# VectorE's order of work in the mixed attention heads: maxima first, row sums and pair splits one step later, a quarter of the next weights split early

## The reference, cut to what matters

```
x += diff_attention(rms_norm(x)) ; x += sq_relu_mlp(rms_norm(x))      # layer 0
k, v = shared_kv(x)
x += swa_sink_attention(rms_norm(x), k, v) ; x += sq_relu_mlp(...)    # layer 1

# diff_attention, 8 heads, S = 1024 rows in 8 blocks of 128; per head:
q, k = rms_norm of each 64 wide half of h @ w_qkv;  v = 128 wide
p_c = softmax(q_c k_c^T - slope*dist, chunk-causal)        # c = 0, 1
o = (p_0 - lam * p_1) @ v ;  o = rms_norm(o) * (1 - lambda_init)
```

## Time and profile before

| | us |
|---|---|
| median of 3 runs | 2393.85 (2392.53 to 2394.03) |
| the profiled execution | 2394.06 |
| its span, first to last instruction | 2392.3 |
| start of the first and of the last projection matmul into `proj` (layer 0) | 46.1 and 522.5 |
| PE busy in the span | 2231.4 (93%) |
| DVE busy | 1591.2 (67%) |
| ACT busy | 1156.5 (48%) |
| POOL busy | 832.6 (35%) |

### The profile page before, as it was taken

One profiled execution on the slowest core, in us unless ns is written; L12 is line 12 of the kernel. 1 busy time (PEld: TensorE's weight loads), 2 busy tenths in 40 slices (PEclk: granted clock), 3 DMA queues, 4 the chain that ended last, 5 costly groups with the idle time before them and its releaser, 6 DMA issues.

```text
span 2392.3 us, 36506 instructions
## 1 busy us (share of the span) xinstructions
PE 2231.4 (93%) x11916; PEld 1910.2 (80%) x11916; DVE 1591.2 (67%) x3173; ACT 1156.5 (48%) x2476; POOL 832.6 (35%) x1461
## 2 busy tenths in 40 slices
PE   6999899986999999999999889998999999899998
PEld 5888788884778888777788888887878888788777
DVE  5677677776376666677766457886576666776773
ACT  4455555553354555534444246664455545543342
POOL 2333222335462222323335245553552222332331
PEclk9999999997999999999999899997999999999999
DMA  6011000001324444744552200003334444763452
GB/s 194 28 28 28 27 27 27 1 19 36 124 87 150 146 145 146 281 156 157 176 176 89 71 19 19 18 1 96 120 102 145 145 148 159 257 237 97 136 178 84
DMA packets 186756, 255.86 MB, mean 107 GB/s; under 512 B 15072, under 2 KB 135904, under 8 KB 181984
## 3 DMA queue, kind: packets, MB, share of 16 engines
q1 hardware_dynamic: 186592, 253.82, 31.9%
HBM read 174.09 MB, written 79.69 MB: 106 GB/s over the span
## 4 chain that ended last, share of the span: by engine, by line
PE 66%; DVE 18%; issue 8%; ACT 5%; DVEq 1%; POOLq 1%; DMA 0%; POOL 0%; ACTq 0%; SPq 0%
PE score L1814 42%; PE trb L1814 13%; PE proj L1814 5%; PE pv L1814 4%; ACT p L946 3%; DVE xop L1324 3%; DVE p L1451 3%; DVE w_op L1324 1%; PE trb L2141 1%; DVE wa_lo L1324 1%; DVE p L1470 1%; DVE coef_a L1465 1%; DVE xT L1550 1%; DVE stat_m L1421 1%; DVE nm_a L1456 1%
## 5 line engine op out<-in xcount | busy, mean ns | idle before, releaser
L1814 PE MATMUL score<-xop,w_op 128*128 128x512 f32 x3840 | 895.0, 392 | 25.2 <-DVE xop L1324 11.3
L1814 PEld LDWEIGHTS score<-xop,w_op 128*128 128x128 f32 x3840 | 721.7, 189 | 185.4 <-issue 36.4
L788 POOL TENSOR_TENSOR w_quad<-w_quad,w_sum 128x512 f32<-128x512 f32 x64 | 99.5, 1555 | 809.5 <-DVE w_op L1324 809.5
L1814 PE MATMUL trb<-xop,w_op 128*128 128x512 f32 x1536 | 363.5, 392 | 4.9 <-DVE w_op L1324 2.0
L1814 PEld LDWEIGHTS trb<-xop,w_op 128*128 128x128 f32 x1536 | 288.5, 188 | 68.5 <-issue 5.2
L912 ACT ACTIVATE w_op<-w_quad 128x512 fp32r<-128x512 f32 (+1 forms) x336 | 216.2, 645 | 247.2 <-PE score L1814 165.6
L1324 DVE TENSOR_TENSOR w_op<-w_quad,w_op 128x512 fp32r<-128x512 f32 (+1 forms) x336 | 286.5, 856 | 43.5 <-ACT w_op L912 43.5
L1550 DVE TENSOR_TENSOR xT<-score,xT 128x512 f32<-128x512 f32 x160 | 109.8, 686 | 157.6 <-PE score L1814 150.5
L1814 PE MATMUL proj<-wa_hi,a_hi 128*128 128x384 f32 x480 | 166.0, 346 | 9.8 <-DVE v_parts L1325 5.3
L946 ACT ACTIVATE p<-p,nm_a,slopes 128x128 f32<-128x128 f32 (+7 forms) x124 | 106.5, 860 | 140.2 <-DVE nm_a L1456 140.1
L1814 PE MATMUL score<-a_hi,w_op 128*128 128x512 f32 x512 | 162.0, 397 | 3.8 <-DVE w_op L1324 3.8
(11 more groups left out here) (256 smaller groups left out, 4505.7 us busy)
## 6 DMA issues: line engine op xcount, KB each, us to landing
xop<-u_dram SPq DMA_DIRECT2D x112, 512.0 KB, 5.9
u_dram<-quad SPq DMA_DIRECT2D x32, 1536.0 KB, 9.6
w_quad<-in_mlp_w_up SPq DMA_DIRECT2D x64, 512.0 KB, 5.3
w_quad<-in_mlp_w_down SPq DMA_DIRECT2D x64, 512.0 KB, 5.0
wa_raw<-in_a_w_qkv SPq DMA_DIRECT2D x96, 128.0 KB, 2.4
quad<-xT_dram SPq DMA_DIRECT2D x32, 256.0 KB, 4.2
xT_dram<-xs SPq DMA_DIRECT2D x32, 256.0 KB, 2.8
u_dram<-quad SPq DMA_DIRECT2D x32, 256.0 KB, 3.8
```

What stands on the lines that cost most here:

```text
L788: return pool.tensor_tensor(out, x, y, ALU.subtract)
L1814: return nc.tensor.matmul(out, a, b, start=start, stop=stop, **kw)
```

## The change

VectorE's `head`: the row sums of block s move from behind the split of v in step s to step s+1, between the low part of the transposed weights and `mix`, as a function `row_sums`. `take_outputs` moves from the end of even steps to the same place in the odd step after it. In steps 2 and 4 `low_pair` of pairs 1 and 3 stands there too, and in step 2 `o_factors`. Pairs 5 and 7 are split right behind the split of v of their own step. In step 0 the low part of the transposed weights goes ahead of the maxima. A wait on `mixed` is added ahead of the second maximum, as `p1` is one buffer.

The weights: the first quarter gets a second place, `wa_even`, for heads with `par` = 1, and is split at the end of step 2; the three others stay at the end of step 7. ScalarE's list follows: squares of outputs of the last two blocks move to step 1 of the next head, pair and weights at s = 7 go behind the copies. TensorE's list is the same but for `wa_rows`, which picks the place. The last head and head -1 take what the moves leave over.

```diff
+        def wa_rows(part, pair, even):
+            if even and pair == 0:
+                return wa_even[:, part, :, :]
+            return (wa_hi, wa_lo)[part][:, 2 * pair:2 * pair + 2, :]
...
@@ ScalarE @@
+            def wa_split(hq, even, first=0, end=4):
                 for i in range(first, end):
+                    if i == 0 and (not isinstance(hq, int) or hq > 1):
+                        act.wait_ge(qkv_ready, (hq - 1) * NB)
+                    if i == max(first, 1) and (not isinstance(hq, int) or hq > 0):
+                        act.wait_ge(qkv_ready, hq * NB)
                     act.wait_ge(wa_in[i], hq * 48 + 48)
...
+                    squares = tail if s == 1 else attn and s in (3, 5)
+                    if squares:
+                        act.wait_ge(red_done, t + NB)
+                        if s == 1:
+                            square_outputs(h * 4 - 1, 1 - par, 4)
+                            act.drain()
                         square_outputs(h * 4 + s // 2, 1 - par if s == 1 else par, (s - 3) % NB)
...
+                    urgent = attn and s in (5, 7)
+                    if urgent:
                         high_pair(uses, h, s, par)
+                    if s == NB - 1 and more:
+                        wa_split(h + 2, par == 0, 1, 4)
+                    if squares:
+                        act.drain()
+                    if not isinstance(h, int) or h >= 0 or s:
+                        act.wait_ge(red_done, t + NB)
+                    act.wait_ge(qkv_copied, t + NB + 1)
+                    nc.scalar.activation(sq_a[:, :], qk2[:, s % 4, :], ACT.Square).then_inc(sq_done, 1)
+                    if ("pair", s) in uses and not urgent:
                         high_pair(uses, h, s, par)
+                    if s == 2 and more:
+                        wa_split(h + 2, par == 0, 0, 1)
...
@@ VectorE @@
                 for s in range(NB):
                     t = h * NB + s
+                    if attn and s:
                         maxima(h, s, 0)
                     for i in range(2):
                         if ("lag", s, i) in uses:
                             low_wT(uses["lag", s, i], i, (s - 1) % NB, wt_use(h, s, i))
+                    if attn and s == 0:
+                        maxima(h, s, 0)
+                    if s % 2 and ("lag", s - 1, 0) in uses:
+                        take_outputs(t - 2, 1 - par if s == 1 else par, (s - 3) % NB)
+                    if s and attn:
+                        row_sums(h, s - 1)
+                    elif tail:
+                        row_sums(h - 1, NB - 1)
+                    if s in (2, 4) and ("pair", s - 1) in uses and attn:
+                        low_pair(uses, h, s - 1, par)
+                    if s == 2 and tail:
+                        o_factors(h, 1 - par)
                     if attn:
                         mix(h, s, par, 0)
+                    dve.wait_ge(qkv_copied, t + NB + 1)
+                    low(v_parts[1 - par][:, s, 1, :], ...).then_inc(qkv_free, 1)
+                    if not attn:
+                        row_sums(h, s)
+                    if ("pair", s) in uses and (s in (5, 7) or not attn):
                         low_pair(uses, h, s, par)
+                    if s in (2, NB - 1) and more:
+                        wa_split(h + 2, par == 0, *((0, 1) if s == 2 else (1, 4)))
...
@@ maxima @@
+                    if c and isinstance(h, int) and h == NH - 1 and s:
                         dve.wait_ge(mixed, t - 1)
+                    elif c and (not isinstance(h, int) or h or s):
+                        dve.wait_ge(mixed, t)
...
@@ VectorE last_head @@
+                    if s == 0:
+                        row_sums(h - 1, NB - 1)
                     mix(h, s, par, s % 2)
```

More of the change, by code:

```diff
@@ L993, in head @@
                         exps(h, s, par, 0)
[L994 to L998, removed]
-                        square_outputs(h * 4 + s // 2, 1 - par if s == 1 else par, (s - 3) % NB)
-                    if at_end:
-                        high_pair(uses, h, s, par)
-                        if more:
-                            wa_split(h + 2, 0, 1)
@@ L1004, in head @@
[L1004 to L1025, removed]
+                    squares = tail if s == 1 else attn and s in (3, 5)
+                    if squares:
+                        act.wait_ge(red_done, t + NB)
+                        if s == 1:
+                            square_outputs(h * 4 - 1, 1 - par, 4)
+                            act.drain()
+                        square_outputs(h * 4 + s // 2, 1 - par if s == 1 else par, (s - 3) % NB)
@@ new lines, in head @@
+                    act.wait_ge(qkv_ready, t + NB + 1)
+                    if s == 0 and tail:
+                        act.wait_ge(pv_ready, h * NB)
+                    rows = qkv_bank(h, s)
+                    copy(v_parts[1 - par][:, s, 0, :], rows[:, 256:384], row_r[:, s:s + 1])
+                    copy(qk2[:, s % 4, :], rows[:, 0:256]).then_inc(qkv_copied, 1)
+                    urgent = attn and s in (5, 7)
+                    if urgent:
+                        high_pair(uses, h, s, par)
@@ L1045, in square_outputs @@
                 last.then_inc(o_squared, 1)
-            wa_split(0)
+            wa_split(0, True)
             for i in range(4):
@@ L1433, in head @@
-                    if ("pair", s) in uses and not (s == NB - 1 and attn):
-                        low_pair(uses, h, s, par)
-                    if s == 1 and tail:
-                        o_factors(h, 1 - par)
-                    if s % 2 == 0 and ("lag", s, 0) in uses:
-                        take_outputs(t - 1, 1 - par if s == 0 else par, (s - 2) % NB)
-                    if s == NB - 1 and more and not attn:
-                        wa_split(h + 2)
+                    dve.wait_ge(qkv_copied, t + NB + 1)
@@ L1944, in head @@
                             last = three(qkv_bank(h, s)[:, 0:384], (a_hi[:, k, tok], a_lo[:, k, tok]),
-                                         (wa_hi[:, k, :], wa_lo[:, k, :]), k == 0, k == KC - 1)
+                                         tuple(wa_rows(part, k // 2, par == 1)[:, k % 2, :] for part in range(2)),
+                                         k == 0, k == KC - 1)
                         last.then_inc(qkv_ready, 1)
```

62 lines of the change are left out of this document (26 added, 36 removed).

## The result

The changed kernel takes 2367.62 us (median of 4 runs, 2366.28 to 2367.95) where the kernel before takes 2393.84 (4 runs, 2392.53 to 2394.03): a ratio of 0.9891, 95% interval 0.9873 to 0.9908, so 26 us faster. The forecast was 2365.5. The profiled execution has a span of 2364.6 us for 2392.3.

The account below looks back on a forecast made before the run. VectorE's chain was taken as the bound, with TensorE close behind. Seven heads save 30.5 us, less 1.4, plus 0.7, makes 29.8, taken as 28.3 for signalling: 2394.1 becomes 2365.8, median 2365.5 us, range 2358 to 2380.

Parts of the forecast that it names:

- the gap filled: VectorE's idle time awaiting exponentials, 10.3 us a head: 9.0 filled, but the gain limited by TensorE's idle 4.1.
- The floor of 58.5 us: TensorE's time for head 3 without its waits: 63.5 less 4.1, then less 0.9 for overlapping matmuls.
- Rival B: TensorE's floor is 59.4 us and two waits are 0.5 larger: 10 us less gain, 2375; chance 0.12.
- (a): Wait ahead of the projection of block 1, behind the split of v: 0.37 us a head stays.
- (b): Step 2, now VectorE's heaviest: 5.9 us against TensorE's some 6.0, so some 0.2 us of new wait.
- (c): Step 7, the longest chain: VectorE's 7.1 us fits TensorE's 7.7, with about 0.4 to spare after signalling.
- (d): Head's end: VectorE's work falls from 7.9 to 4.9 us; waits of 1.5 for wT_lo and 0.54 for v's split go.
- (e): Waits of steps 3 and 6, 1.2 and 0.6 us, for mix 2 and the bank of pair 5, go.
- Rival A: GpSimd's long operations hold the mix of step 2 or 7: two of 1.04 us lose 14 us, 2380; chance 0.13.
- Head 2: Head with the loop's jump back: 63.8 us against 69.4, keeping 3.15 us idle and 1.7 for slow clock.
- Head -1: ScalarE makes three weight quarters before its squares, and low quarters end later: cost 1.4 us once.
- Last head: Row sums leave the time before the first maxima, squares enter ScalarE's step 1: gain 0.7 us, bounds -1.5 and +1.5.

Follow-up runs that it names:

- e9a: Kernel before with 16 of the 192 projection matmuls of a head left out; 2393.06 us, one run.
- e2: Changed kernel with VectorE splitting pair 3 ahead of the row sums in step 4; 2360.43 us, 0.9854 of before.
- e4: Changed kernel with GpSimd's multiply of the outputs cut from 128x1024 to 128x8 in heads 0 to 6; 2361.91 us, 0.9862 of before.
- e7: Kernel before with only the early weight quarter added, split in step 2; 2395.09 us, 0.9989 of before.
- e3: Changed kernel without the early quarter, all four weight quarters split at the end of step 7; 2371.05 us, 0.9902 of before.
- e8: Changed kernel with head -1's weights behind squares and pair, pair 3 split ahead of step 4's row sums, and no early quarter; 2361.60 us, 0.9850 of before.
- e1: Changed kernel with ScalarE making the squares and the pair before the three weight quarters in head -1; 2363.96 us, 0.9864 of before.
- e5: Changed kernel with the row sums of block 7 ahead of the last head's first maxima, as before; 2373.15 us, one run.
- e9b: Changed kernel with 16 of the 192 projection matmuls of a head left out; 2362.77 us, one run.

## Why the prediction was right, and where its steps were not

**VectorE set the pace, and the gap filled is not the gain.** Right. e9a: 2.8 us less of TensorE's work a head changed nothing before. The reciprocal's waits fell from 10.3 us a head to 10.2 for all of them, and of 9.0 us filled some 3 came out as time, since TensorE took over. Two of the signs that I had named did not come, though. TensorE's idle time in head 3 is 2.2 us (1.54, 0.25 and 0.38), not under 1. And the chain that ended last in that window runs through GpSimd's norms, with 60.9% of it issue, and not through TensorE; since no wait of TensorE in the mixed heads is for GpSimd, and GpSimd is busy 23 of 60.8 us, that chain says little of the pace here.

**The floor of 58.5 us.** Right to some 0.4 us. After's head 3 gives 58.6 and e2's 58.5, with the waits as the trace shows them. With the 0.2 us that I had added to each of five waits before, e2's two would give 58.1; so the 0.2 us are not shown by themselves, only that the floor and the one wait of 0.37 together come to what I used. Rival B's 59.4 falls: e2's heads take less than that with their waits.

**(a) to (e).** (a), the 0.37 us, stayed. (b), a new wait of 0.2 us at step 2, did not come; one of 0.25 us in step 7, which I did not have, did, so the sum of the period kept its size by chance. Apart from that (c) held: in step 7 VectorE itself waits for scores. (d) held: wT_lo releases nothing in the mixed heads but at the jump back (0.4 us). (e) failed. I wrote that the waits of steps 3 and 6 go because both were late only through VectorE, and so they did. But I costed pair 3 as filling of step 4's gap (1.95 us) and did not ask who waits for the bank that it frees. The outputs' transposes do, 1.1 to 1.5 us in heads 1 to 5, 7.4 us in all. That is the larger part of 60.4 to 60.75 us where I had 59.05; head 0, which has no outputs to transpose, came out as predicted (58.03).

**Rival A.** A hold did fall on the path, 1.34 us (1.57 less 0.23) on nm_a in step 4, where I had looked only at mixes and coefficients in steps 2 and 7. It costs nothing in e2, where the bank is freed early enough. The Trainium skill, page "SBUF — State Buffer", section "SBUF: two separate sides", states an exclusive lock of one shared port pair between GpSimd's operations and those of VectorE that have two SBUF inputs or run in a two-port mode. The trace agrees in kind: 1.57 us beside the long multiply, 0.23 without it (e4). nm_a has one tensor and one scalar per partition as inputs, so it isn't plainly of the kind that the prediction quoted, and no run here shows in which mode it ran. That GpSimd's multiply holds it is shown; that it does so by the port is inferred, from the two ends 0.02 us apart.

**Head 2.** Wrong in my disfavour by 2.6 us. I kept 3.15 us of idle and 1.7 of slow clock at the jump back; TensorE idled 0.41 and the clock stayed at 1.00. VectorE's gap there is 1.34 us for 3.67. What stands in front of it differs: 2.69 us of weight splits in after, short row sums before. With the row sums still in front and the early quarter added (e7) the gap is 4.00; in the nine kernels with the new order it is 1.07 to 1.34, in the three with the old 3.67 to 4.00. VectorE's timeline of after, and then of e3:

```profile
265.78 1.29 DVE L1333 TENSOR_TENSOR wT_lo<-trb,wT_hi 128x512 fp32r<-128x512 f32 x2 [1.34 <-issue]
```

```profile
266.65 1.29 DVE L1327 TENSOR_TENSOR wT_lo<-trb,wT_hi 128x512 fp32r<-128x512 f32 x2 [1.28 <-issue]
```

That queued work covers the pause is what I thought, but e3 and e8 speak against it in this simple form: they have 3.56 us of splits in front, 0.87 more, and their gaps are 1.28 and 1.21, no shorter than the others'. What stands first behind the jump differs too, a low part of weights in the new order and the first maxima in the old. So the order of the two sides of the jump is worth 2.3 to 2.9 us of VectorE's gap; why stays open.

**Head -1.** The term that was mis-sized most: -4.1 us for -1.4. I had the squares behind three weight copies and the wait inside the projection, and the delay itself was sized about right: the matmul of 83.53 has six ahead of it, so it stands for a start at 82.5 us, 1.6 later than the 80.88 before. What I left out is that the wait of 3.57 us inside the projection would be followed by 5 us at half clock, 2.5 us (e1). (The 3.04 us for four copies that the sum uses are all four in one row of the trace; the earlier trace rows shows only the first, 0.84.)

**Last head.** +0.67 for +0.7. The row sums' gain was largely taken by a wait of 3.38 us for GpSimd's q and k; e5 shows that the old place of the row sums does no better.

**Sum.** Heads 23.2 for 28.3: head -1 2.7 worse, head 2 2.6 better, the five heads 1, 3, 4, 5 and 6 together 6.6 worse, and the 1.5 for signalling has no row behind it and was not found in the trace as a term of its own. The span fell by 27.7 us, near the 28.3, only because 4.5 us more fell in layer 1, where the clock read higher; the median fell by 26.2. Without these 4.5 us the time would have been about 2370 to 2372.

## What to carry to other kernels

When work is moved into a gap, ask of each piece what it frees and who waits for that: the pair's split filled its gap as planned and held a bank 1.1 us too long, which cost 7 us until it was put first in the same gap. Once VectorE and TensorE are within some 1 us of each other, a piece that was worth next to nothing alone (the early quarter, 0.9989) is worth about 4 us in the right company, so try pieces again after the next wait is removed. Cut the program at the reach of the change before you believe the total: a sixth of this gain lies outside it.

## What the runs showed of the hardware that was not expected

An instruction of 128x2 on VectorE (nm_a) took 1.57 us beside GpSimd's multiply of 128x1024 (1.90 us), 0.76 beside one of 128x512 (1.04 us), and 0.23 alone. At the loop's jump back VectorE paused 3.67 to 4.00 us with short work in front and 1.07 to 1.34 with 2.7 us of weight splits in front, and no less with 3.6 us of them (e3, e8). TensorE's granted clock was 1.00 behind idle stretches of 3.21 us (before) and 1.61 us (e1) at the same place, and 0.50 behind one of 3.57 (after) and 0.51 behind one of 3.21 (e8); at step 4 of e9b it was 0.54 to 0.61 behind one of 1.98 us, and behind one of 1.94, at step 4 of head 1 of the same run, 1.00. So the length of the idle stretch alone does not decide it, and what does isn't settled here.
